# Partition sums of the conditioning products: a block transpose and a sum on the vector engine and three fold matmuls a layer, in place of two ones-column matmuls for each job

## The chip, the cores and the metric

The kernel runs on one core of one Trainium2 chip, as one launch. The metric is the device time of that launch in microseconds (us); lower is better. The median of before is 2668.92 us over 3 runs (2668.68 to 2669.47).

## The reference, cut to what matters

Two layers of a decoder trunk over 512 tokens of width 1024. In each layer three sub-layers (a gated feed-forward block, a mixer, a second gated feed-forward block) are modulated by a shift, a scale and a gate that come from one conditioning vector `c` of 1024 numbers:

```
c_act = jax.nn.silu(c)
for l in range(DEPTH):
    mod = c_act @ w_ada[l] + b_ada[l]
    sh1, sc1, g1, sh2, sc2, g2, sh3, sc3, g3 = jnp.split(mod, N_MOD, axis=-1)
    h = modulate(rmsnorm(x, norm_ffn1[l]), sh1, sc1)
    x = x + 0.5 * g1[:, None, :] * swiglu(h, ffn1_w_up[l], ffn1_w_down[l])
    h = modulate(rmsnorm(x, norm_mix[l]), sh2, sc2)
    x = x + g2[:, None, :] * hybrid_mixer(h, ...)
    h = modulate(rmsnorm(x, norm_ffn2[l]), sh3, sc3)
    x = x + 0.5 * g3[:, None, :] * swiglu(h, ffn2_w_up[l], ffn2_w_down[l])
```

`w_ada[l]` is 1024 x 9216 in float32. The change is only in how `c_act @ w_ada[l]` is summed.

## The kernel before, in words

The five engines have instruction streams written out by hand and meet at semaphores (`wait_ge`, `then_inc`); nothing reorders them. All activations are held with the 1024 features over the 128 partitions and the 512 tokens along the free axis. Each projection is made of units: one unit is one output tile of 128 features. Its weights arrive in `raw[s]` (s is 0 or 1, two units are a pair), the scalar engine rounds them to `Whi[s]` (L433), the vector engine makes the rest `Wlo[s]` (L703), and TensorE multiplies three times for each of the input tiles (L1179, L1180, L1181: high by high, high weights by low activations, low weights by high activations). A unit of the up projection has 8 input tiles (24 matmuls), one of the down projection 11 (33 matmuls).

A feed-forward block (`ffn(l, f)` on every engine, f is 0 for the first and 1 for the second) has two halves of `HALF` = 11 up pairs and then 4 down pairs. After an up pair VectorE multiplies the two banks (L810) and makes the low part of the product (L813); after each unit of a down pair it adds the bank into the residual stream (L787, `add_gated`).

The conditioning product is cut into jobs of 256 columns: 36 for a layer. The first 8 of layer 0 are made ahead of the layers, in code that the change leaves alone. The other 28 of a layer ride in the first feed-forward block: one behind each of the 11 up pairs and the first 3 down pairs, in both halves; and the first 8 of layer 1 ride in the second feed-forward block of layer 0. So 2 x 28 + 8 = 64 jobs are concerned. A job has these parts:

- the scalar engine issues the load of 1 MB of `w_ada` into `ada_raw` (L450);
- VectorE (`ada_sum_job`) multiplies its 8 row tiles by the columns of `c_act` and adds them into `ada_acc`, 128 partitions x 256 (L713 once, L715 seven times); what is left is a sum over the 128 partitions;
- TensorE (`ada_job`, placed behind the next pair of units) makes that sum with two matmuls of `ada_acc` by a column of ones, into two columns of PSUM (L1205);
- VectorE (`ada_store_job`, ahead of the sum of the next job) adds the bias and puts the two columns into `mod` (L726).

`mod` is read by `norm` (shift and scale) and by `halve_gate` (gate, L793). The last down pair of the second half is followed by the sum of squares of the next norm on TensorE (`sum_squares`, L1142), the inverse root on VectorE (L735 to L743), its spread over the partitions on TensorE (`spread_rstd`, L1212) and the norm itself (L778, L772).

## Time and profile before

| | |
|---|---|
| median of 3 runs | 2668.92 us (2668.68 to 2669.47) |
| span of the profiled execution | 2665.5 us from its first to its last instruction |
| TensorE matmuls busy | 2561.8 us, 96% of the span |
| VectorE busy | 1378.9 us, 52% |
| ScalarE busy | 849.9 us, 32% |
| GpSimd busy | 96.5 us, 4% |
| mean granted TensorE clock | 0.979 of full speed |

The profiled execution has its span; no device time of its own is listed beside it. The span leaves out what lies before the first and behind the last instruction: the median of the runs is 3.4 us above it. In rows of TensorE the ends of matmuls are modelled and overlap, so steps are best read from start to start.

### The profile page before, as it was taken

The page shows a single profiled execution, that of the slowest core. Times are in us where ns is not written, and L with a number is a line of the kernel's source. Part 1 is how long each engine was busy: PE and PEld are TensorE (multiplying, and loading weights), DVE is VectorE, ACT ScalarE, POOL GpSimd, SP SyncE. Part 2 cuts the span into 40 slices and gives each one's busy share as a digit, 9 for nine tenths or more (in the row PEclk, how much of TensorE's full clock was granted, in tenths as well). Part 3 has the DMA queues.
Part 4 walks back from the last instruction along what each step waited for, and adds up shares of the span by engine and source line. Part 5 has one row for each costly group of instructions (what it writes and reads, how often), then busy time and mean ns, then how long its engine had stood idle before and what let it go on. Part 6 is the DMA issues. An engine that isn't in the chain of part 4 may idle for free.

```text
span 2665.5 us, 36408 instructions
## 1 busy us (share of the span) xinstructions
PE 2561.8 (96%) x12039; PEld 2101.2 (79%) x12039; DVE 1378.9 (52%) x2175; ACT 849.9 (32%) x1276; POOL 96.5 (4%) x76
## 2 busy tenths in 40 slices
PE   6999999999999989999989999999999999899998
PEld 5888887877778878888868888877777888788886
DVE  7665665467644446433356656645665343433333
ACT  2321222444422334222222222234443223332222
POOL 3000001000000010000100000100000001000001
PEclk7999998999999999999989999999999999999999
DMA  6664664211123436423336656532111343233332
GB/s 220 181 194 137 186 179 132 79 56 55 56 63 100 129 90 186 120 85 99 106 103 180 181 160 183 164 103 64 55 55 48 94 128 101 71 102 95 95 109 65
DMA packets 494947, 307.08 MB, mean 115 GB/s; under 512 B 8904, under 2 KB 488472, under 8 KB 494232
## 3 DMA queue, kind: packets, MB, share of 16 engines
q1 hardware_dynamic: 427288, 239.03, 30.8%
q10 hardware_dynamic: 67584, 67.12, 7.8%
q8 instruction: 39, 0.64, 0.1%
q14 instruction: 36, 0.29, 0.0%
HBM read 299.82 MB, written 6.29 MB: 115 GB/s over the span
## 4 chain that ended last, share of the span: by engine, by line
PE 81%; DVE 9%; ACT 4%; issue 3%; DMA 1%; DVEq 0%; ACTq 0%; SPq 0%
PE ps_proj L1179 25%; PE ps_proj L1181 24%; PE ps_proj L1180 24%; ACT sb_scratch L534 2%; DVE sb_small L899 1%; DVE sb_w_lo L703 1%; DVE sb_scratch L896 1%; PE ps_mid L1322 1%; PE ps_mid L1324 1%; PE ps_mid L1323 1%; DVE sb_scratch L919 1%; ACT sb_w_hi L433 1%; PE ps_mid L1205 1%; PE ps_mid L1383 1%; DVE sb_scratch L924 1%
## 5 line engine op out<-in xcount | busy, mean ns | idle before, releaser
L1179 PE MATMUL ps_proj<-sb_h_hi,sb_w_hi 128*128 128x512 f32 x2048 | 815.0, 398 | 18.6 <-DVE sb_h_lo L772 14.4
L1181 PE MATMUL ps_proj<-sb_h_hi,sb_w_lo 128*128 128x512 f32 x2048 | 801.8, 392 | 0.0
L1180 PE MATMUL ps_proj<-sb_h_lo,sb_w_hi 128*128 128x512 f32 x2048 | 801.2, 391 | 0.0
L703 DVE TENSOR_TENSOR sb_w_lo<-sb_raw,sb_w_hi 128x1024 fp32r<-128x1024 f32 (+1 forms) x388 | 500.9, 1291 | 462.1 <-ACT sb_w_hi L433 454.0
L433 ACT ACTIVATE sb_w_hi<-sb_raw 128x1024 fp32r<-128x1024 f32 (+1 forms) x388 | 430.3, 1110 | 811.9 <-PE ps_proj L1181 755.3
L1179 PEld LDWEIGHTS ps_proj<-sb_h_hi,sb_w_hi 128*128 128x128 f32 x2048 | 386.9, 189 | 114.5 <-DVE sb_h_lo L772 20.2
L1181 PEld LDWEIGHTS ps_proj<-sb_h_hi,sb_w_lo 128*128 128x128 f32 x2048 | 386.8, 189 | 82.8
L1180 PEld LDWEIGHTS ps_proj<-sb_h_lo,sb_w_hi 128*128 128x128 f32 x2048 | 387.6, 189 | 78.0
L1179 PE MATMUL ps_proj<-sb_a_hi,sb_w_hi 128*128 128x512 f32 x1088 | 426.5, 392 | 0.0
L1181 PE MATMUL ps_proj<-sb_a_hi,sb_w_lo 128*128 128x512 f32 x1088 | 424.3, 390 | 0.0
L1180 PE MATMUL ps_proj<-sb_a_lo,sb_w_hi 128*128 128x512 f32 x1088 | 423.8, 390 | 0.0
L1181 PEld LDWEIGHTS ps_proj<-sb_a_hi,sb_w_lo 128*128 128x128 f32 x1088 | 204.6, 188 | 43.0
L1180 PEld LDWEIGHTS ps_proj<-sb_a_lo,sb_w_hi 128*128 128x128 f32 x1088 | 204.8, 188 | 42.2
L1179 PEld LDWEIGHTS ps_proj<-sb_a_hi,sb_w_hi 128*128 128x128 f32 x1088 | 204.6, 188 | 41.7
L715 DVE SCALAR_TENSOR_TENSOR sb_scratch<-sb_scratch,sb_c_act 128x256 f32<-128x256 f32 x448 | 217.2, 485 | 16.0
L787 DVE SCALAR_TENSOR_TENSOR sb_x_or_values<-ps_proj,sb_half_gate,sb_x_or_values 128x512 f32 (+1 forms) x80 | 60.1, 751 | 289.3 <-PE ps_proj L1181 288.7
L810 DVE TENSOR_TENSOR sb_scratch<-sb_scratch,ps_proj 128x512 f32<-128x512 f32 x88 | 60.5, 687 | 206.5 <-PE ps_proj L1181 206.5
L477 ACT ACTIVATE sb_scratch<-ps_proj 128x512 f32<-128x512 f32 x88 | 52.7, 599 | 300.6 <-PE ps_proj L1181 300.5
L394 POOL TENSOR_TENSOR sb_scratch<-sb_scratch 128x512 f32<-128x512 f32 x35 | 62.2, 1778 | 1998.8 <-ACT sb_scratch L444 1998.2
L534 ACT ACTIVATE sb_scratch<-sb_scratch,sb_small 128x256 f32<-128x256 f32 x128 | 63.0, 493 | 0.0
L813 DVE TENSOR_TENSOR sb_a_lo<-sb_scratch,sb_a_hi 128x512 f32 (+1 forms) x88 | 60.2, 684 | 0.0
L444 ACT ACTIVATE sb_scratch<-sb_x_or_values 128x512 f32<-128x512 f32 (+1 forms) x56 | 34.6, 621 | 74.9 <-DVE sb_x_or_values L787 55.2
(148 smaller groups left out, 1765.8 us busy)
## 6 DMA issues: line engine op xcount, KB each, us to landing
sb_raw<-in_ffn_w_up SPq DMA_DIRECT2D x176, 512.0 KB, 3.8
sb_scratch<-in_w_ada ACTq DMA_DIRECT2D x128, 512.0 KB, 4.3
sb_raw<-in_w_in SPq DMA_DIRECT2D x100, 512.0 KB, 3.8
sb_raw<-in_ffn_w_down SPq DMA_DIRECT2D x64, 704.0 KB, 4.5
sb_raw<-in_w_branch_swa SPq DMA_DIRECT2D x16, 512.0 KB, 3.6
sb_raw<-in_w_branch_ret SPq DMA_DIRECT2D x16, 512.0 KB, 3.6
sb_raw<-in_w_out SPq DMA_DIRECT2D x16, 512.0 KB, 3.6
sb_scratch<-in_w_ada SPq DMA_DIRECT2D x14, 512.0 KB, 7.9
```

The costliest lines, as they stand in the source:

```text
L394: pool.tensor_tensor(square_sum, square_sum, squares[:, k % 2, :], ALU.add).then_inc(sq_used, 1)
L433: act.activation(Whi[s][:, 0:n], raw[s][:, 0:n], ACT.Copy).then_inc(hi_ready, 1)
L477: act.activation(side, pA[0][:, :], ACT.Silu).then_inc(bank_free[0], 1)
L534: last = act.activation(p, p, ACT.Exp, bias=neg_m[w][:, n:n + 1], scale=HD ** -0.5, accum_out=row_sum[w][:, n:n + 1])
L703: dve.tensor_tensor(Wlo[s][:, 0:n], raw[s][:, 0:n], Whi[s][:, 0:n].bitcast(F), ALU.subtract).then_inc(lo_ready, 1)
L715: ins = dve.scalar_tensor_tensor(ada_acc, ada_raw[s][:, k % 4, :], col, ada_acc, ALU.mult, ALU.add)
L787: dve.scalar_tensor_tensor(XV[:, m, :], pA[s][:, :], half_gate[:, bass.ds(m, 1)], XV[:, m, :], ALU.mult, ALU.add).then_inc(bank_free[s], 1)
L810: dve.tensor_tensor(work, side, pA[1][:, :], ALU.mult).then_inc(bank_free[1], 1)
L813: dve.tensor_tensor(Alo[:, i, :], work, Ahi[:, i, :].bitcast(F), ALU.subtract).then_inc(act_lo, 1)
L1179: pe.matmul(bank, Whi[s][:, w], hi, start=first, stop=False)
L1180: pe.matmul(bank, Whi[s][:, w], lo, start=False, stop=False)
L1181: return pe.matmul(bank, Wlo[s][:, w], hi, start=False, stop=last)
```

## The change

In a job, VectorE now goes on behind its eight products: it transposes `ada_acc` in blocks of 32 x 32 into `ada_turned`, and sums each run of 32 (`reduce_sum`), which gives 8 columns for the job in `ada_part`. Each of these holds, on partition p, a partial sum over one group of 32 partitions. `ada_part` gathers the columns of many jobs. A fold matmul (`fold_jobs`) multiplies them by a constant 128 x 128 matrix `fold_rows` that has a one wherever two partitions agree modulo 32. So the four groups are added and each partition gets the result. The store (`ada_store`) picks the right column for each group of 32 partitions in four additions.

There are three folds in layer 0 and two in layer 1: `GATE_FOLD` for the 11 jobs of the up pairs of the first half (88 columns), between the two units of the first down pair; `REST_FOLD` for the other 17 (136 columns), between the two units of the last down pair of the second half, ahead of `sum_squares`; and in layer 0 `NEXT_FOLD` for the 8 jobs of the next layer (64 columns), behind the ninth up pair of the second feed-forward block. The constants grow by 128 columns (64 KB), which the first load brings in.

```diff
-            def ada_sum_job(l, q):
+            def ada_sum_job(l, q, slot):
...
                         ins.then_inc(ada_step, 1)
                         dve.wait_ge(ada_step, 6 * no + k - s + 1)
 
-            def ada_store_job(l, q, to, bias):
-                dve.wait_ge(ada_col, job_no(l, q) + 1)
-                dve.tensor_tensor(mod[:, bass.ds(2 * to, 2)], pC, vcols[:, bass.ds(64 + bias, 2)],
-                                  ALU.add).then_inc(mod_done, 1)
+                dve.wait_ge(ada_used, 2 * no + 4)
+                dve.transpose(ada_turned, ada_acc).then_inc(ada_turn, 1)
+                dve.wait_ge(ada_turn, no + 1)
+                dve.reduce_sum(ada_part[:, bass.ds(8 * slot, 8)], ada_turned.rearrange("p (j r) -> p j r", r=32), AX.X).then_inc(ada_part_done, 1)
+
+            def ada_store(fold, q, n, bias):
+
+                dve.wait_ge(ada_fold, fold + 1)
+                for a in range(4):
+                    rows = slice(32 * a, 32 * (a + 1))
+                    last = dve.tensor_tensor(mod[rows, 2 * q:2 * (q + n)], pC[rows, 0:8 * n].rearrange("p (x a) -> p x a", a=4)[:, :, a],
+                                             vcols[rows, bass.ds(64 + bias, 2 * n)], ALU.add)
+                last.then_inc(mod_done, 1)
...
                     if f == 0:
-                        up(0, UP_UNIT, lambda n: ada_sum_job(l, q0))
-                        with st.loop(1, HALF - 1, 0) as i:
-                            up(i, UP_UNIT, both_jobs)
-                        up(HALF - 1, DOWN_UNIT, both_jobs)
+                        with st.loop(0, HALF - 1, 0) as i:
+                            up(i, UP_UNIT, own_job)
+                        up(HALF - 1, DOWN_UNIT, own_job)
+                        if half == 0:
+                            ada_store(fold_no(l, GATE_FOLD), FIRST_JOBS, GATE_JOBS, MOD_TILES * l + 2 * FIRST_JOBS)
...
+                            if f == 0 and half and s == 0 and isinstance(j, int):
+                                rest = JOBS - FIRST_JOBS - GATE_JOBS
+                                ada_store(fold_no(l, REST_FOLD), JOBS - rest, rest, MOD_TILES * l + 2 * (JOBS - rest))
...
-            def ada_job(l, q):
-                pe.wait_ge(ada_used, 2 * job_no(l, q) + 4)
-                pe.wait_ge(mod_done, job_no(l, q) + 1)
-                for n in range(2):
-                    last = pe.matmul(pC[:, n:n + 1], ada_acc[:, P * n:P * (n + 1)], ones, start=True, stop=True)
-                last.then_inc(ada_col, 1)
+            def fold_jobs(fold, end, slot, n):
+
+                pe.wait_ge(ada_part_done, end)
+                pe.matmul(pC[:, 0:8 * n], fold_rows, ada_part[:, 8 * slot:8 * (slot + n)], start=True, stop=True).then_inc(ada_fold, 1)
...
-                        if f == 0:
-                            ada_job(l, q0 + i - 1)
...
-                        with pe.Fori(0, KT // 2) as j:
+                        down(0, lambda: None if f else fold_jobs(fold_no(l, GATE_FOLD), job_no(l, FIRST_JOBS + GATE_JOBS), 0, GATE_JOBS))
+                        with pe.Fori(1, KT // 2) as j:
                             down(j, lambda: None)
                     else:
-                        add_pairs(3 * l + (3 if f else 1), down)
+                        add_pairs(3 * l + (3 if f else 1), down, lambda: None if f else fold_jobs(
+                            fold_no(l, REST_FOLD), job_no(l, JOBS), GATE_JOBS, JOBS - FIRST_JOBS - GATE_JOBS))
```

What moves, in the order of instructions. On TensorE, at the end of the loop over the up pairs of the first half, before (L1205 is the job's two matmuls, L1202 and L1203 its two waits, L1250 the loop):

```order
L1181 MATMUL ps_proj<-sb_h_hi,sb_w_lo 128x512
L1202 ISA
L1203 REGISTER_ALU
L1205 MATMUL ps_mid<-sb_consts,sb_scratch 128x1 x2
L1250 REGISTER_ALU
L1250 COMPARE_AND_BRANCH
```

and in the changed kernel at the same place (L1198 to L1200 are the three products, L1271 the loop):

```order
L1200 MATMUL ps_proj<-sb_h_hi,sb_w_lo 128x512
L1271 REGISTER_ALU
L1271 COMPARE_AND_BRANCH
L1209 ISA
L1210 REGISTER_ALU
L1216 ISA
```

The pair is followed at once by the branch and the next pair; the job and its two waits are gone. The first fold stands between the two units of the first down pair (L1222 is its wait):

```order
L1198 MATMUL ps_proj<-sb_a_hi,sb_w_hi 128x512
L1199 MATMUL ps_proj<-sb_a_lo,sb_w_hi 128x512
L1200 MATMUL ps_proj<-sb_a_hi,sb_w_lo 128x512
L1222 ISA
L1223 MATMUL ps_mid<-sb_scratch,sb_consts 128x88
```

One matmul of 88 columns, with one wait, stands where two units followed each other directly.

On VectorE, in the loop over the up pairs, before, between the low part of the product (L813) and the first product of the job (L713):

```order
L813 ISA [waits act_hi]
L813 TENSOR_TENSOR sb_a_lo<-sb_scratch,sb_a_hi 128x512
L725 ISA
L726 ISA [waits ada_col]
L726 ISA
L726 TENSOR_TENSOR sb_mod<-ps_mid,sb_vector_cols 128x2
L711 ISA
L713 TENSOR_SCALAR sb_scratch<-sb_scratch,sb_c_act 128x256 [waits ada_in0]
```

and in the changed kernel at the end of the job (L729 is the last of the products, L739 the block transpose, L741 the sum), where before the loop ended behind the last product:

```order
L729 SCALAR_TENSOR_TENSOR sb_scratch<-sb_scratch,sb_c_act 128x256 [waits ada_step]
L738 REGISTER_ALU
L739 STREAM_TRANSPOSE sb_scratch<-sb_scratch 128x256 [waits ada_used]
L741 ISA [waits ada_turn]
L741 TENSOR_REDUCE sb_scratch<-sb_scratch 128x8
L250 REGISTER_ALU
L250 COMPARE_AND_BRANCH
```

The store of the job before is gone from the head of the job, and two instructions that each wait for the one before stand at its end. Behind the last job of the first half VectorE waits for the fold and stores 22 columns for each group of 32 partitions (L748), ahead of halving the gate (L816):

```order
L741 TENSOR_REDUCE sb_scratch<-sb_scratch 128x8 [waits ada_turn]
L748 ISA [waits ada_fold]
L748 TENSOR_TENSOR sb_mod<-ps_mid,sb_vector_cols 32x22
L748 ISA
L748 TENSOR_TENSOR sb_mod<-ps_mid,sb_vector_cols 32x22
L748 ISA
L748 TENSOR_TENSOR sb_mod<-ps_mid,sb_vector_cols 32x22
L748 ISA
L748 TENSOR_TENSOR sb_mod<-ps_mid,sb_vector_cols 32x22
L815 REGISTER_ALU
L816 TENSOR_SCALAR sb_half_gate<-sb_mod 128x8 [waits mod_done]
```

Before, only the halving stood here, with columns that had been stored several jobs earlier.

## Rows read from the trace of the kernel before

**Rows 1.** The page: span, busy time of TensorE, chain that ended last by engine
```profile
span 2665.5 us, 36408 instructions
...
PE 2561.8 (96%) x12039; PEld 2101.2 (79%) x12039; DVE 1378.9 (52%) x2175; ACT 849.9 (32%) x1276; POOL 96.5 (4%) x76
...
PE 81%; DVE 9%; ACT 4%; issue 3%; DMA 1%; DVEq 0%; ACTq 0%; SPq 0%
```

**Rows 2.** Groups of instructions of TensorE: busy us, mean ns, idle before
```profile
L1205 PE MATMUL ps_mid<-sb_consts,sb_scratch 128*128 128x1 f32 x256 | 31.9, 228 | 0.0
...
L1205 PEld LDWEIGHTS ps_mid<-sb_consts,sb_scratch 128*128 128x128 f32 x256 | 38.3, 190 | 5.1
```

**Rows 3.** Timeline of TensorE around one job: start us, us, engine, line
```profile
129.89 0.39 PE L1181 MATMUL ps_proj<-sb_h_hi,sb_w_lo 128*128 128x512 f32 x1
130.12 0.50 PE L1205 MATMUL ps_mid<-sb_consts,sb_scratch 128*128 128x1 f32 x4
130.48 0.48 PE L1179 MATMUL ps_proj<-sb_h_hi,sb_w_hi 128*128 128x512 f32 x1
130.79 0.39 PE L1180 MATMUL ps_proj<-sb_h_lo,sb_w_hi 128*128 128x512 f32 x1
```

**Rows 4.** Timeline of VectorE over one pair with a job
```profile
119.15 0.69 DVE L810 TENSOR_TENSOR sb_scratch<-sb_scratch,ps_proj 128x512 f32<-128x512 f32 x1 [2.70 <-PE ps_proj L1181]
...
122.23 3.61 DVE L715 SCALAR_TENSOR_TENSOR sb_scratch<-sb_scratch,sb_c_act 128x256 f32<-128x256 f32 x7
126.60 1.23 DVE L703 TENSOR_TENSOR sb_w_lo<-sb_raw,sb_w_hi 128x1024 fp32r<-128x1024 f32 x1 [0.76 <-ACT sb_w_hi L433]
130.52 0.69 DVE L810 TENSOR_TENSOR sb_scratch<-sb_scratch,ps_proj 128x512 f32<-128x512 f32 x1 [2.70 <-PE ps_proj L1181]
```

**Rows 5.** Timeline of VectorE over one pair without a job
```profile
1190.08 0.69 DVE L810 TENSOR_TENSOR sb_scratch<-sb_scratch,ps_proj 128x512 f32<-128x512 f32 x1 [2.76 <-PE ps_proj L1181]
...
1200.96 0.69 DVE L810 TENSOR_TENSOR sb_scratch<-sb_scratch,ps_proj 128x512 f32<-128x512 f32 x1 [2.76 <-PE ps_proj L1181]
```

**Rows 6.** Groups of instructions of VectorE by shape
```profile
L899 DVE TENSOR_REDUCE sb_small<-sb_scratch 128x4 f32<-128x1024 f32 x32 | 39.0, 1220 | 1.1
...
L1035 DVE TENSOR_TENSOR sb_scratch<-ps_mid,sb_consts 128x256 f32<-128x256 f32 x8 | 3.3, 417 | 2.0 <-PE ps_mid L1377 2.0
```

**Rows 7.** Timeline of VectorE, last job of the first up stage
```profile
190.74 0.15 DVE L726 TENSOR_TENSOR sb_mod<-ps_mid,sb_vector_cols 128x2 f32<-128x2 f32 x1
190.81 0.34 DVE L713 TENSOR_SCALAR sb_scratch<-sb_scratch,sb_c_act 128x256 f32<-128x256 f32 x1
191.19 3.61 DVE L715 SCALAR_TENSOR_TENSOR sb_scratch<-sb_scratch,sb_c_act 128x256 f32<-128x256 f32 x7
```

**Rows 8.** Timeline of TensorE, last matmul of that up stage
```profile
186.76 0.39 PE L1181 MATMUL ps_proj<-sb_h_hi,sb_w_lo 128*128 128x512 f32 x1
```

**Rows 9.** Timeline of VectorE, last job of the second half
```profile
423.00 1.32 DVE L713 TENSOR_SCALAR sb_scratch<-sb_scratch,sb_c_act 128x256 f32<-128x256 f32 x1
424.35 3.61 DVE L715 SCALAR_TENSOR_TENSOR sb_scratch<-sb_scratch,sb_c_act 128x256 f32<-128x256 f32 x7
```

**Rows 10.** Timeline of TensorE, last matmul before that job
```profile
419.54 0.39 PE L1181 MATMUL ps_proj<-sb_a_hi,sb_w_lo 128*128 128x512 f32 x1
```

**Rows 11.** Timeline of TensorE, sum of squares behind the second half
```profile
437.91 1.32 PE L1142 MATMUL ps_small<-sb_consts,sb_scratch 128*128 128x1 f32 x8 [0.35 <-ACT sb_scratch L444]
```

**Rows 12.** Timeline of TensorE, two waits in the mixer
```profile
529.44 0.92 PE L1285 MATMUL ps_mid<-sb_scratch 64*128 64x256 f32 x6 [2.16 <-DVE sb_small L908]
...
540.26 0.70 PE L1285 MATMUL ps_mid<-sb_scratch 64*128 64x256 f32 x4 [1.54 <-DVE sb_small L908]
```

**Rows 13.** Windows of TensorE behind these: us, busy (count), PEclk, DMA, GB/s
```profile
530.80:534.00 3.20, 3.20 (x9) 0.50 0.00 0
...
541.00:544.00 3.00, 3.00 (x16) 1.00 0.02 5
```

**Rows 14.** DMA issues: KB each, median us to landing
```profile
sb_consts<-in_consts SPq DMA_DIRECT2D x1, 1536.0 KB, 9.7
```

More of the change, by code:

```diff
@@ L815, in up @@
                             jobs(i)
-                    def store_job(n):
-                        ada_store_job(l, q0 + n, q0 + n, MOD_TILES * l + 2 * (q0 + n))
-                    def both_jobs(n):
-                        store_job(n - 1)
-                        ada_sum_job(l, q0 + n)
-                    def next_layers_jobs(n, store=True, add=True):
-                        with dve.If(l < DEPTH - 1):
-                            if store:
-                                ada_store_job(l, JOBS + n - 1, n - 1, nc.s_assert_within(
-                                    MOD_TILES * (l + 1) + 2 * (n - 1), MOD_TILES, MOD_TILES * DEPTH - 2,
-                                    skip_runtime_bounds_check_because="the last layer does not come here"))
-                            if add:
-                                ada_sum_job(l, JOBS + n)
@@ new lines, in next_layers_job @@
+                    def next_layers_job(n):
+                        with dve.If(l < DEPTH - 1):
+                            ada_sum_job(l, JOBS + n, n)
+                    if f == 0:
+                        with st.loop(0, HALF - 1, 0) as i:
[3 more added lines that the diff above has]
+                            ada_store(fold_no(l, GATE_FOLD), FIRST_JOBS, GATE_JOBS, MOD_TILES * l + 2 * FIRST_JOBS)
+                    elif half == 0:
+                        with st.loop(0, FIRST_JOBS, 0) as i:
+                            up(i, UP_UNIT, next_layers_job)
+                        up(FIRST_JOBS, UP_UNIT)
+                        with dve.If(l < DEPTH - 1):
+                            ada_store(fold_no(l, NEXT_FOLD), 0, FIRST_JOBS, nc.s_assert_within(
+                                MOD_TILES * (l + 1), MOD_TILES, MOD_TILES * (DEPTH - 1),
+                                skip_runtime_bounds_check_because="the last layer does not come here"))
@@ L1217, in _, with add_pairs, between @@
             first_columns(4).then_inc(first_col, 1)
-            def add_pairs(no, pair):
+            def add_pairs(no, pair, fold=lambda: None):
+                def between():
+                    fold()
+                    sum_squares(no, 0)
                 with pe.Fori(0, KT // 2 - 1) as j:
                     pair(j, lambda: None)
-                pair(KT // 2 - 1, lambda: sum_squares(no, 0))
+                pair(KT // 2 - 1, between)
                 for part in (1, 2):
```

39 lines of the change are left out of this document (22 added, 17 removed).

## The prediction

> **What bounds the kernel now.** I read the page first: TensorE's matmuls are busy for 96% of a span of 2665.5 us, and 81% of the chain that ended last is its own work [rows 1]. So what TensorE no longer does counts in full, as long as nothing else comes to hold it. Then I read the groups of TensorE for the job's matmuls: 256 records with no idle time before them [rows 2]. There are 64 jobs, so a job is four records (each float32 matmul shows as two), and TensorE never waited for a job's sum. The timeline shows how they stand in the stream: between the last product of one pair at 129.89 and the first of the next at 130.48 [rows 3].
>
> What a job costs is best read from start to start of one event that recurs once a pair. The product of the two banks on VectorE does: 119.15 to 130.52 with a job, 11.37 us; 1190.08 to 1200.96 without one, 10.88 us [rows 4, 5]. The pair is the same 48 matmuls in both, 0.227 us each. A job costs 0.49 us, more than the 0.36 us that its rows seem to take, since the next products start a little later too (0.31 us between the first two [rows 3]).
>
> **What the change removes.** Of the 64 jobs, 62 stand between two units. The last of each layer's stands ahead of the sum of squares, and there TensorE is held by ScalarE a moment later (0.35 us idle before 437.91 [rows 11]); removing its 0.36 us only lengthens that wait, so I count those two at nothing. The 62 give 62 x 0.49 = 30.4 us. That the pair really falls to 10.88 us without its job, and isn't held there by VectorE, ScalarE or loads, I take from the stages without jobs [rows 5], and check below against VectorE's longer job.
>
> The 64 stores on VectorE (0.15 us, of which the next instruction sees 0.07: 190.74 to 190.81 [rows 7]) are replaced by 5 x 4 small ones. VectorE is idle when they run, so they count only where they stand ahead of something late; see the folds.
>
> **What it adds to VectorE.** The trace has no block transpose. The nearest rows of 256 elements are the product with a constant table, 0.42 us [rows 6], and the scalar product, which goes faster, 0.34 us [rows 7]. I take 0.42; 0.34 is the lower bound, and the 1.22 us of a sum over 1024 elements [rows 6] the upper. Those two rows lie on one line, (1.22 - 0.42)/768 = 1.04 ns for each element, so I price the new sum of 256 at 0.42 us too. Each of the two waits for the instruction before it, about 0.03 us (seven dependent products take 3.61 us). Together a job grows by 0.90 us, 0.73 to 1.70 with the bounds.
>
> The Trainium skill (VectorE: DVE Perf Modes, The three transpose paths) gives 311 ns for a block transpose of 128 x 128 in bf16; an estimate from it, with one more element for each of its cycles, is 0.44 us for 256 columns, if float32 costs no more. The sum below would be 0.1 us worse by it. No row here shows it.
>
> Does that hide? In an up pair the job's products end at 122.23 + 3.61 = 125.84. VectorE then idles until 126.60, when ScalarE's half of the next weights is ready, and makes the low half until 127.83 [rows 4]. With the store gone, the longer job ends at 126.67; in the changed kernel ScalarE is 0.49 us earlier, so the low half starts then and ends at 127.90. The next pair would want these weights about 0.4 us ahead of its product of banks at 119.15 + 10.88 = 130.03, at 129.6. So 1.7 us are left, or 0.9 at the upper bound. The weights of the second unit are made ahead of the job. Down pairs are 4 us longer. So 60 of the 64 longer jobs cost nothing; the four that a fold waits for do.
>
> **The folds on TensorE.** A fold is one float32 matmul, two records instead of four, with 88, 136 or 64 columns instead of one. Half a job, 0.25 us, is the lower bound; a whole job, 0.49, the upper. I take 0.35, since more columns lengthen it a little. Five folds: 1.8 us.
>
> **The waits ahead of the folds.** This is what the change puts in the path. The first fold needs the sum of the eleventh job, and stands only one unit of 33 matmuls behind the last up pair. That pair's last product starts at 186.76 [rows 8]; without the job in between, the fold's first weight load (0.19 us, and it carries the wait [rows 2]) would start 33 x 0.227 = 7.48 us later, at 194.24. On VectorE the products of that job end at 191.19 + 3.61 = 194.80 [rows 7], 0.07 earlier without the store; plus 0.90 for transpose and sum and 0.1 for the signal gives 195.7. TensorE waits 1.5 us. The second fold is alike: the last product ahead of it is at 419.54 [rows 10], its load would start at 427.02. The last job's first product takes 1.32 us instead of 0.34, as it does in the down pairs of this half only, and its products end at 427.96 [rows 9]; so the sum is ready at 427.96 - 0.07 + 1.0 = 428.9, a wait of 1.9 us. Both stand in both layers: 2 x (1.5 + 1.9) = 6.8 us. The third fold, in layer 0 only, stands one whole pair of 10.88 us behind its last job, and doesn't wait.
>
> Queued behind these waits on TensorE is the second unit of the down pair, so the wait counts in full. On VectorE the wait for the fold (ahead of the four stores) holds the first addition into the residual stream and then the low half of the next weights: they come some 3 us later than now, and TensorE wants them at the end of the second unit, 7.5 us behind the fold. Hidden.
>
> **The start.** The first load of constants grows by 64 KB. At the rate of the big one, 1536 KB in 9.7 us [rows 14], that is 0.4 us of the transfers that the start waits for; between 0 and 0.4 I take 0.2.
>
> **The sum.** 30.4 - 1.8 - 6.8 - 0.2 = 21.6 us. The span becomes 2643.9; with the 3.4 us by which the median of the runs stands above the span, 2668.9 - 21.6 = 2647.3.
>
> **Rivals.**
>
> 1. *The clock falls at the fold waits.* In the mixer a wait of 2.16 us ahead of 529.44 is followed by a stretch at half clock (1.2 GHz) that covers 530.8 to 534.0; one of 1.54 us ahead of 540.26 is not, 541 to 544 is at full clock [rows 12, 13]. My waits, 1.5 and 1.9, lie between. The Trainium skill (TensorE: Matmul & The Clock Gate, The HAM clock gate) has the array's clock set by how busy it was just before; the trace agrees. A stretch like that one, 3.2 us at half clock, loses 1.6 us. If all four waits do it: 6.4 us more, 2653.7.
> 2. *No wait at the folds.* If the transpose and sum were nearly free and the jobs ran earlier, the 6.8 us would stay: 2640.5. Against it: the old job alone ends at 194.80, already 0.56 us later than the fold's load at 194.24.
> 3. *The pair does not get shorter.* Without the job TensorE would wait for weights instead, since each pair then moves its 1 MB of weights and the job's 1 MB in 10.88 us where rows 5 moved only the first. Then the 30.4 us don't come, while TensorE's waits would also cover the folds: 2668 to 2671, no change. Against it: TensorE's records show no wait behind any job pair now, and the job-less pairs leave VectorE 2.76 us idle.
> 4. *Slower: VectorE becomes the bound of the up pairs.* If transpose and sum took x us instead of 0.90, each job beyond x = 0.90 + 1.7 = 2.6 holds its pair. All is given back when 21.6 = 4 (x - 0.9) + 60 (x - 2.6), at x = 2.8 us; at 3.0, 2647.3 + 8.4 + 24.0 = 2679.7. It needs a block transpose of over 2.3 us, nearly twice the dearest row of four times the size.
>
> **How the numbers follow.** The forecast as summed has 0.68. Its own range: the transpose at its bounds changes four waits by -0.3 to +3.2; the folds by -0.5 to +0.7; the start by 0.2 either way. The starts of the six stages behind a norm run at half clock for a while, and how long depends on when they start; 21 us earlier they start at another moment, which I can't place: 2 us either way. Together 2644 to 2653.5. Rival 1 has 0.12 and ends in the same place or just above. Rival 2 has 0.07, rival 3 0.05, rival 4 0.04, and 0.04 is left for what I don't see. A range from 2641 to 2655 leaves out the last three, most of rival 2 and little else.
>
> A measurement of this kernel can tell about 0.2%, 5.3 us. Forecast, rivals 1 and 2 are all faster: with part of the rest 0.92. Within 0.2%: 0.04. Slower: 0.04.
>
> **What would show each step.** The product of the banks every 10.88 us in all up pairs; the busy time of VectorE 50 us higher (64 x 0.84, less the stores); the block transpose near 0.42 us; two groups of TensorE waits for the sum on VectorE, four in all, 1.5 and 1.9 us; five folds of two records. Wrong would be the prediction if pairs with a job stay above 10.88 us, if the transpose takes over 1 us, or if the clock's half-speed stretches grow in number within the down stages.

## The result and the profile after

The changed kernel takes 2647.45 us (median of 4 runs, 2646.18 to 2649.83), the kernel before in the same series 2669.01 (4 runs, 2668.68 to 2669.47). The ratio is 0.992, with a 95% interval of 0.9908 to 0.9932: faster by 0.8%, with the whole interval below 1. The prediction was 2647.3.

The page of the changed kernel, which answers to [rows 1]:

```profile
span 2645.3 us, 35817 instructions
...
PE 2538.1 (96%) x11793; PEld 2077.2 (79%) x11793; DVE 1431.3 (54%) x2259; ACT 852.0 (32%) x1276; POOL 94.4 (4%) x76
```

TensorE has 246 matmul records less (256 gone, 10 new) and is busy for 23.7 us less. VectorE is busy for 52.4 us more. The span fell by 20.2 us, in one execution of each; the medians of the runs are 21.6 us apart.

The groups of VectorE and TensorE for the new instructions, by shape (busy us, mean ns, idle before):

```profile
L739 DVE STREAM_TRANSPOSE sb_scratch<-sb_scratch 128x256 f32<-128x256 f32 x64 | 28.5, 446 | 2.2
...
L741 DVE TENSOR_REDUCE sb_scratch<-sb_scratch 128x256 f32 x60 | 25.2, 420 | 9.7 <-DVE sb_scratch L739 9.7
...
L1223 PE MATMUL ps_mid<-sb_scratch,sb_consts 128*128 128x136 f32 x4 | 1.0, 331 | 3.3 <-DVE sb_scratch L741 3.3
L1223 PE MATMUL ps_mid<-sb_scratch,sb_consts 128*128 128x88 f32 x4 | 0.9, 309 | 2.2 <-DVE sb_scratch L741 2.2
```

The block transpose takes 0.446 us and the sum 0.420 us. The timeline of VectorE over one pair with a job answers to [rows 4]:

```profile
105.59 0.69 DVE L833 TENSOR_TENSOR sb_scratch<-sb_scratch,ps_proj 128x512 f32<-128x512 f32 x1 [2.01 <-PE ps_proj L1200]
...
108.47 3.61 DVE L729 SCALAR_TENSOR_TENSOR sb_scratch<-sb_scratch,sb_c_act 128x256 f32<-128x256 f32 x7
112.11 0.45 DVE L739 STREAM_TRANSPOSE sb_scratch<-sb_scratch 128x256 f32<-128x256 f32 x1
112.71 0.42 DVE L741 TENSOR_REDUCE sb_scratch<-sb_scratch 128x256 f32 x1 [0.15 <-DVE sb_scratch L739]
113.24 1.23 DVE L717 TENSOR_TENSOR sb_w_lo<-sb_raw,sb_w_hi 128x1024 fp32r<-128x1024 f32 x1
116.47 0.69 DVE L833 TENSOR_TENSOR sb_scratch<-sb_scratch,ps_proj 128x512 f32<-128x512 f32 x1 [2.01 <-PE ps_proj L1200]
```

The product of the banks (L833) comes at 105.59 and again at 116.47, 10.88 us later, where it took 11.37 [rows 4]: now a pair with a job is as long as one without [rows 5]. VectorE still sits idle for 2.01 us ahead of it, waiting for TensorE.

The timeline of TensorE at the first fold, with the row of the last product ahead of it:

```profile
188.45 0.39 PE L1200 MATMUL ps_proj<-sb_a_hi,sb_w_lo 128*128 128x512 f32 x1
189.94 0.46 PE L1223 MATMUL ps_mid<-sb_scratch,sb_consts 128*128 128x88 f32 x2 [1.10 <-DVE sb_scratch L741]
190.18 0.48 PE L1198 MATMUL ps_proj<-sb_a_hi,sb_w_hi 128*128 128x512 f32 x1
190.50 0.39 PE L1199 MATMUL ps_proj<-sb_a_lo,sb_w_hi 128*128 128x512 f32 x1
```

and at the last fold, up to where the clock has fallen:

```profile
414.47 0.39 PE L1200 MATMUL ps_proj<-sb_a_hi,sb_w_lo 128*128 128x512 f32 x1
416.54 0.50 PE L1223 MATMUL ps_mid<-sb_scratch,sb_consts 128*128 128x136 f32 x2 [1.67 <-DVE sb_scratch L741]
416.87 0.95 PE L1161 MATMUL ps_small<-sb_consts,sb_scratch 128*128 128x1 f32 x8
...
418.63 0.63 PE L1198 MATMUL ps_proj<-sb_a_hi,sb_w_hi 128*128 128x512 f32 x1
419.06 0.63 PE L1199 MATMUL ps_proj<-sb_a_lo,sb_w_hi 128*128 128x512 f32 x1
```

What a fold costs with its wait is best read from starts: from 188.45 to the second product behind the fold at 190.50 are 2.05 us, where two steps of the stream would be 0.45, so the first fold costs 1.60. From 414.47 to the sum of squares at 416.87 are 2.40, where one step would be 0.23, so the last costs 2.17. The number in brackets is less (1.10 and 1.67), since the weight load of the fold is in the cost and not in the wait.

Behind the last fold the products start 0.43 us apart instead of 0.23. The windows of TensorE (us; busy and count of PE, PEld, DVE, ACT, POOL; granted clock; DMA share; GB/s) show why; the first row is behind the last fold of layer 0, the second follows it, and the third is behind the last fold of layer 1:

```profile
418.90:422.10 3.20, 3.20 (x9) 2.43 (x9) 0.08 (x1) 0.00 (x0) 0.00 (x0) 0.57 0.54 164
422.30:425.00 2.70, 2.70 (x13) 2.21 (x12) 0.00 (x0) 0.00 (x0) 0.00 (x0) 1.00 0.00 0
...
1709.30:1712.30 3.00, 3.00 (x10) 2.34 (x9) 0.28 (x2) 0.00 (x0) 0.00 (x0) 0.57 0.55 174
```

TensorE is busy without a gap in all three, but in the first and third the granted clock is near half: 9 or 10 matmuls are done there, where full clock does some 15. By the spacing of the products (0.43 us against 0.23), each such stretch loses about 1.6 us, an estimate. Behind the first fold, with a cost of 1.60 us, there is none.

The stages of both traces, in us, from the first spread of 1/rms on TensorE to the next; the start is all that comes ahead, and the time at half clock is the sum of the trace's clock records at that level:

| | start | ffn 1, layer 0 | mixer 0 | ffn 2, layer 0 | ffn 1, layer 1 | mixer 1 | ffn 2, layer 1 | half clock |
|---|---|---|---|---|---|---|---|---|
| before | 52.8 | 388.9 | 317.3 | 381.5 | 388.3 | 314.4 | 374.1 | 116.2 |
| after | 51.6 | 380.6 | 317.1 | 377.2 | 379.6 | 316.9 | 373.7 | 123.1 |
| change | -1.2 | -8.3 | -0.2 | -4.3 | -8.7 | +2.5 | -0.4 | +6.9 |

(The rest of each mixer, 216.5, and the end, 15.1, stayed within 0.2.) Three stages hold the jobs and are shorter by 21.3 us. The mixer of layer 1, in which nothing was changed, is 2.5 us longer.

### The profile page after: what moved, and what is told of

The parts are those of the page before. It is cut to its first block, busy times and chain, and to the rows that moved or that the text cites. A ratio compares the mean times of both kernels' runs of the same rounds, so it can differ in the third digit from the quotient of the medians.

```text
span 2645.3 us, 35817 instructions
## 1 busy us (share of the span) xinstructions
PE 2538.1 (96%) x11793; PEld 2077.2 (79%) x11793; DVE 1431.3 (54%) x2259; ACT 852.0 (32%) x1276; POOL 94.4 (4%) x76
## 4 chain that ended last, share of the span: by engine, by line
PE 79%; DVE 11%; ACT 5%; issue 3%; DMA 1%; DVEq 0%; ACTq 0%; SPq 0%
PE ps_proj L1198 24%; PE ps_proj L1199 24%; PE ps_proj L1200 24%; ACT sb_scratch L548 2%; DVE sb_w_lo L717 2%; DVE sb_small L918 1%; DVE sb_scratch L915 1%; PE ps_mid L1339 1%; ACT sb_w_hi L447 1%; PE ps_mid L1340 1%; PE ps_mid L1341 1%; DVE sb_scratch L938 1%; PE ps_mid L1400 1%; DVE sb_scratch L943 1%; DVE sb_scratch L729 1%
## 5 line engine op out<-in xcount | busy, mean ns | idle before, releaser
L1198 PE MATMUL ps_proj<-sb_h_hi,sb_w_hi 128*128 128x512 f32 x2048 | 810.3, 396 | 16.9 <-DVE sb_h_lo L795 12.7
L1200 PE MATMUL ps_proj<-sb_h_hi,sb_w_lo 128*128 128x512 f32 x2048 | 801.1, 391 | 0.0
L1198 PEld LDWEIGHTS ps_proj<-sb_h_hi,sb_w_hi 128*128 128x128 f32 x2048 | 386.7, 189 | 114.6 <-DVE sb_h_lo L795 18.4
L1200 PEld LDWEIGHTS ps_proj<-sb_h_hi,sb_w_lo 128*128 128x128 f32 x2048 | 386.9, 189 | 81.7
L1198 PE MATMUL ps_proj<-sb_a_hi,sb_w_hi 128*128 128x512 f32 x1088 | 426.8, 392 | 0.0
L1200 PE MATMUL ps_proj<-sb_a_hi,sb_w_lo 128*128 128x512 f32 x1088 | 425.9, 391 | 0.0
L1200 PEld LDWEIGHTS ps_proj<-sb_a_hi,sb_w_lo 128*128 128x128 f32 x1088 | 205.7, 189 | 43.3
L1198 PEld LDWEIGHTS ps_proj<-sb_a_hi,sb_w_hi 128*128 128x128 f32 x1088 | 205.8, 189 | 42.9
L729 DVE SCALAR_TENSOR_TENSOR sb_scratch<-sb_scratch,sb_c_act 128x256 f32<-128x256 f32 x448 | 217.3, 485 | 16.0
L833 DVE TENSOR_TENSOR sb_scratch<-sb_scratch,ps_proj 128x512 f32<-128x512 f32 x88 | 60.5, 688 | 181.7 <-PE ps_proj L1200 181.4
```

Of the source, the lines that this page charges most:

```text
L729: ins = dve.scalar_tensor_tensor(ada_acc, ada_raw[s][:, k % 4, :], col, ada_acc, ALU.mult, ALU.add)
L833: dve.tensor_tensor(work, side, pA[1][:, :], ALU.mult).then_inc(bank_free[1], 1)
L1198: pe.matmul(bank, Whi[s][:, w], hi, start=first, stop=False)
L1200: return pe.matmul(bank, Wlo[s][:, w], hi, start=False, stop=last)
```

## The experiments

Three theories on the size and place of the result: (A) the gain is TensorE's time for the jobs, 0.49 us each, and the waits at the folds are its price; (B) the folds' waits cost more than they show, since the clock falls behind them; (C) VectorE's longer job is near the bound. All ratios are to the kernel before, timed on the same chip.

**e0: the changed kernel again**, for comparison with e1 to e3.

> The changed kernel once more, beside its variants on one chip. My account (the 62 jobs leave TensorE's path, four waits ahead of the folds and two half-clock stretches are the price): 2647.4 us again, within 1.5, as the others of this call are read against it. A rival that calls the first result a lucky draw has it 5 us or more away.

Measured: 2647.48 us (5 runs, 2646.14 to 2648.67), ratio 0.992 (0.9906 to 0.9933).

**e1: the first fold takes only 4 jobs**, those that the gate needs; the other 24 go to the last fold.

```
-GATE_JOBS = HALF
+GATE_JOBS = 4
```

> The first fold takes only the 4 jobs that the gate needs (32 columns), the last fold the other 24 (192 columns). The first fold then needs a sum that was ready seven pairs earlier. If the wait of the first fold is a real cost on the path: its matmul follows the unit without a wait, about 1.25 us less in each layer, 2.5 us less than the changed kernel, 2645; the last fold and the half-clock stretch behind it stay. Rival (the time is only moved, since VectorE is late at that place anyway and its weights would hold the second unit): no difference, and a wait for low weights appears in the first down pair.

Measured: 2642.98 us (2641.63 to 2644.17), ratio 0.9903 (0.9888 to 0.9918), 4.5 us less than e0. Two rows of TensorE's timeline, the first fold and the last:

```profile
188.80 0.31 PE L1223 MATMUL ps_mid<-sb_scratch,sb_consts 128*128 128x32 f32 x2
...
415.26 0.59 PE L1223 MATMUL ps_mid<-sb_scratch,sb_consts 128*128 128x192 f32 x2 [1.67 <-DVE sb_scratch L741]
```

The first fold has no wait left and costs 0.24 us, so 2 x 1.36 = 2.7 us came from there, as expected. Of the other 1.8 us, about 1.6 are a half-clock stretch that is gone. The last fold still waits for 1.67 us, exactly as in the changed kernel, and yet of the windows behind it only that in layer 1 is at half clock:

```profile
418.70:422.00 3.30, 3.30 (x16) 2.75 (x15) 0.00 (x0) 0.00 (x0) 0.00 (x0) 1.00 0.38 140
1705.40:1708.40 3.00, 3.00 (x8) 2.31 (x7) 0.00 (x0) 0.00 (x0) 0.00 (x0) 0.50 0.59 175
```

The wait in layer 1 is the same 1.67 us. The same wait, with the same work ahead of it, is followed by half clock or not.

**e2: the last fold stands later**, between the second and the third part of the sum of squares, and its store ahead of the inverse root.

```
-                def between():
-                    fold()
-                    sum_squares(no, 0)
...
-                pair(KT // 2 - 1, between)
-                for part in (1, 2):
-                    sum_squares(no, part)
+                pair(KT // 2 - 1, lambda: sum_squares(no, 0))
+                sum_squares(no, 1)
+                fold()
+                sum_squares(no, 2)
```

> The last fold moves behind the last unit, between the second and third part of the sum of squares, where TensorE waits for ScalarE anyway; its store follows the last addition on VectorE. My account: in each layer the excess of 2.17 us at that fold goes, with the half-clock stretch behind it (1.6 us more), so about 7.5 us less than the changed kernel, 2640; the third part of the sum of squares starts no later behind the last unit than now. Rival (what is saved comes back in front of the norm, where fold, store and root would queue): the spread of the root starts 0.5 to 1.5 us later behind the last unit in each layer, and only 4 to 6 us are left.

Measured: 2641.5 us (2639.69 to 2642.2), ratio 0.9896 (0.9881 to 0.9911), 6.0 less than e0. TensorE's timeline at the last fold has no wait for VectorE's sum any more, and the window from the old place of the fold to the norm is at full clock throughout:

```profile
425.52 0.94 PE L1161 MATMUL ps_small<-sb_consts,sb_scratch 128*128 128x1 f32 x8
426.33 0.48 PE L1223 MATMUL ps_mid<-sb_scratch,sb_consts 128*128 128x136 f32 x2
427.27 0.94 PE L1161 MATMUL ps_small<-sb_consts,sb_scratch 128*128 128x1 f32 x7 [0.46 <-ACT sb_scratch L458]
```

```profile
417.00:430.50 13.50, 10.86 (x61) 9.20 (x59) 6.73 (x22) 3.27 (x4) 0.31 (x1) 1.00 0.13 39
```

The two stages of the first feed-forward blocks are 3.2 and 3.8 us shorter than in e0. The whole wait and fold would give 2.17 each, and a half-clock stretch 1.6: 3.8. The 0.6 us that layer 0 lacks lie at the start of the stage, as the table under e3 shows. The rival, that the saving comes back in front of the norm, is out: the spread of the root starts 5.55 us behind the last product in both layers, in e0 and in e2.

**e3: both edits.**

> Both edits: the fold of the gate with 4 jobs only, the last fold behind the last unit. If the two prices are apart from each other they add up: 2.5 and 7.5 us less than the changed kernel, 2637.5; TensorE then shows no wait for the sum on VectorE at any fold. If the clock at the starts of later stages takes its share, up to 3 us of it are lost.

Measured: 2639.87 us (2638.49 to 2640.64), ratio 0.9893 (0.9878 to 0.9908), 7.6 less than e0. No fold waits. The same two stages are 6.1 and 5.3 us shorter than in e0; the waits, folds and stretches account for 1.36 + 3.8 = 5.2 each. In layer 0 the time from the spread to the first product of the banks differs by up to 1.7 us between the traces, for the same instructions. Without it, from the first product of the banks of the first feed-forward block to the next spread, the traces agree with the account within 0.1 us, but for layer 1 of e1 (us):

| | layer 0 | layer 1 | shorter than in e0 | accounted for |
|---|---|---|---|---|
| before | 368.28 | 368.13 | | |
| after | 359.97 | 359.99 | | |
| e0 | 359.99 | 359.95 | | |
| e1 | 357.08 | 359.15 | 2.9, 0.8 | 1.36 + 1.6 = 3.0; 1.36 |
| e2 | 356.20 | 356.20 | 3.8, 3.8 | 3.8 each |
| e3 | 354.81 | 354.80 | 5.2, 5.2 | 5.2 each |

In layer 1 of e1 another half-clock stretch begins 3.6 us ahead of the spread, over the sum of squares, and the spread comes 6.04 us behind the last product instead of 5.55: that is the missing 0.5.

e4 to e7 ran on another chip, on which the kernel before took 2669.03 us instead of 2667.93, so differences to e0 and e3 below are uncertain by about 1 us more.

**e4: the matmuls of the jobs put back.** On the changed kernel, TensorE again makes two float32 ones-column matmuls for each job, at the old places, but on a constant tile, without a wait, into a bank that nobody reads. What the kernel computes stays the same.

```
+            def ones_pair():
+                for n in range(2):
+                    pe.matmul(pM[:, 0, n:n + 1], ident, ones, start=True, stop=True)
```

> The changed kernel with two ones-column matmuls put back on TensorE at each of the old places in the first feed-forward blocks and for the eight jobs of the next layer, on a constant tile into an unused bank, so that they wait for nothing and nobody waits for them. If the gain is the matmuls' own time on TensorE: 62 x 0.49 = 30.4 us more than the changed kernel, 2678, and every pair with a job back at 11.37 us. Rival (part of the gain came from the waits and stores that went with them, on TensorE's queue or on VectorE): less, 10 to 25 us.

Measured: 2675.96 us (10 runs, 2674.48 to 2677.54), ratio 1.0026 (1.0016 to 1.0035): slower than before the change, and 28.5 us above e0. VectorE's timeline has the product of the banks 11.38 to 11.39 us apart:

```profile
107.62 0.69 DVE L833 TENSOR_TENSOR sb_scratch<-sb_scratch,ps_proj 128x512 f32<-128x512 f32 x1 [2.52 <-PE ps_proj L1200]
119.00 0.69 DVE L833 TENSOR_TENSOR sb_scratch<-sb_scratch,ps_proj 128x512 f32<-128x512 f32 x1 [2.52 <-PE ps_proj L1200]
130.39 0.69 DVE L833 TENSOR_TENSOR sb_scratch<-sb_scratch,ps_proj 128x512 f32<-128x512 f32 x1 [2.52 <-PE ps_proj L1200]
```

So two matmuls of one column cost 0.51 us in each pair, although they do next to nothing, and they are the whole gain: 62 x 0.51 = 31.6 us. Less came for two reasons. TensorE arrives 0.5 us later at the folds, and the two cost 1.08 and 1.66 instead of 1.60 and 2.17, which gives back 2.1 us over two layers; and the half-clock stretch behind the last fold of layer 0 is gone, 1.6 us. That would leave 27.9. From the first product of the banks to the spread, layer 0 is 11.0 us and layer 1 12.7 us longer than in e0, where 27 x 0.51 less the folds, and in layer 0 less the stretch, gives 11.1 and 12.7. The clock again treats the two last folds differently: their waits are 1.16 and 1.17 us, and of the windows behind them (layer 1, then layer 0) the first is at half clock:

```profile
1737.20:1740.20 3.00, 3.00 (x8) 2.35 (x8) 0.50 (x3) 0.00 (x0) 0.00 (x0) 0.50 0.59 169
431.50:434.50 3.00, 3.00 (x15) 2.47 (x15) 1.13 (x5) 0.08 (x1) 0.00 (x0) 1.00 0.39 94
```

**e5: e3 and two more block transposes in each job**, each waiting for the one before, so that a job on VectorE grows by 0.96 us.

```
-                dve.transpose(ada_turned, ada_acc).then_inc(ada_turn, 1)
-                dve.wait_ge(ada_turn, no + 1)
+                for turn in range(3):
+                    dve.transpose(ada_turned, ada_acc).then_inc(ada_turn, 1)
+                    dve.wait_ge(ada_turn, 3 * no + turn + 1)
```

> The kernel with both folds moved, and two more block transposes in each job, each behind a wait for the one before: 1.0 to 1.2 us more on VectorE for each of 64 jobs, 64 to 77 us of busy time. My account (in a pair the longer job has 1.4 us of room before the next unit lacks weights, by the changed kernel's trace): no more than 1 us of difference, 2640. Rival (work on VectorE counts in proportion): 2650 or more.

Measured: 2634.8 us (2633.77 to 2635.95), ratio 0.987 (0.9853 to 0.9886). VectorE is busy with block transposes for 57 us more, as its group shows, and the pairs still take 10.88 us, with the idle time ahead of the product of banks down from 2.01 to 1.05:

```profile
L740 DVE STREAM_TRANSPOSE sb_scratch<-sb_scratch 128x256 f32<-128x256 f32 x192 | 85.5, 446 | 6.6
```

```profile
106.18 0.69 DVE L834 TENSOR_TENSOR sb_scratch<-sb_scratch,ps_proj 128x512 f32<-128x512 f32 x1 [1.05 <-PE ps_proj L1201]
...
117.06 0.69 DVE L834 TENSOR_TENSOR sb_scratch<-sb_scratch,ps_proj 128x512 f32<-128x512 f32 x1 [1.05 <-PE ps_proj L1201]
```

From the first product of the banks to the spread both layers take 355.0 us, against 354.8 in e3. The work is hidden, as expected; that the kernel was 5 us faster than e3 was not, and e8 to e10 take it up.

**e6: e3 and four more block transposes.** The same edit with `range(5)`; a job grows by 1.92 us, to 2.97 from the end of the products to the end of the sum.

> The same with four more block transposes, 2.0 to 2.4 us more for each job: beyond the room of 1.4 us. My account: each of the 52 up pairs behind which a job stands now lacks weights by 0.6 to 1.0 us, 30 to 50 us in all, 2670 to 2690, so slower than before the change; TensorE's waits are for the low half of the weights. Down pairs, which are 4 us longer, stay as they are. Rival (the room is larger, up to 2.7 us by the idle time of VectorE in a pair without a job): 2640 still.

Measured: 2656.14 us (2655.02 to 2657.74), ratio 0.9949 (0.9933 to 0.9966), 16.3 above e3. The chosen mechanism is there and the size was missed: 30 to 50 us and a time above that of the kernel before were expected. The four transposes added 1.92 us to a job and not 2.0 to 2.4, and the room was not 1.4 us but about 1.6 (an estimate: 1.92 less the 0.36 below). TensorE's waits have a new line, and its timeline shows one of them:

```profile
PE ps_proj L1199 <- DVE sb_w_lo L717: 13.8, 27, 1.7
```

```profile
117.06 0.39 PE L1201 MATMUL ps_proj<-sb_h_hi,sb_w_lo 128*128 128x512 f32 x1
117.82 0.49 PE L1199 MATMUL ps_proj<-sb_h_hi,sb_w_hi 128*128 128x512 f32 x1 [0.38 <-DVE sb_w_lo L717]
```

TensorE waits for the low half of the weights, which VectorE makes behind the job. Only every other pair does: the product of the banks comes at 106.91, 117.83, 129.40, 140.30, so 10.92, 11.57 and 10.90 us apart. The mean over two pairs is 11.24, 0.36 above 10.88. In the traces the three stages with jobs, from the first product of the banks to the spread, are together 18.6 us longer than in e3.

**e7: the changed kernel and two more block transposes**, with the first and last fold where the change put them.

> The changed kernel with its folds where they are, and two more block transposes in each job. Pairs keep 10.88 us; each of the four fold waits grows by 1.0 to 1.2 us, 4 to 5 us in all. The wait of the first fold is then 2.1 to 2.3 us instead of 1.1: if such a wait is what brings the clock down, half-clock stretches appear behind the first fold too, 1.6 us for each, and the time is 2653 to 2656. Rival (the clock falls behind the last fold for another reason, the sum of squares that follows it): no new stretch behind the first fold, 2651.5 to 2652.5.

Measured: 2660.45 us (6 runs, 2658.28 to 2660.93), ratio 0.9967 (0.9955 to 0.998), 13 above e0 and above both of the expected ranges. The four waits for the sum grew from 5.5 us together to 9.2:

```profile
PE ps_mid L1224 <- DVE sb_scratch L742: 9.2, 4, 2.6
```

The first fold costs 2.46 us now and the last 3.26 and 3.13, so 3.8 of the 13 us are wait. Half clock follows the last fold of layer 0 (for twice as long as in the changed kernel), the first fold of layer 1, and the last fold of layer 1, in this order:

```profile
419.40:426.00 6.60, 6.60 (x22) 5.54 (x22) 2.09 (x6) 0.63 (x1) 0.00 (x0) 0.50 0.28 79
1487.80:1491.00 3.20, 3.20 (x9) 2.42 (x9) 2.28 (x2) 0.00 (x0) 0.00 (x0) 0.50 0.37 120
1716.40:1719.60 3.20, 3.20 (x11) 2.62 (x11) 1.47 (x5) 0.42 (x1) 0.00 (x0) 0.50 0.32 66
```

Behind the first fold of layer 0, with the same cost of 2.46, the clock stays full. So half clock can follow a fold that has no sum of squares behind it, which answers the rival, and need not follow it. The mixers are 0.9 and 2.2 us longer than in the changed kernel, and the time at half clock is 136.6 us against 123.1. The waits, two half-clock stretches more (3.2) and the mixers add up to 10.1 us; the profiled execution, the fastest of the six, has a span 9.6 above that of e0. For the rest of the 13 I have no trace.

**e8, e9, e10: e3 and e5 again, and one more block transpose instead of two**, all on one chip, on where e5's 5 us came from.

> The kernel of e3 unchanged, so that it and e5's kernel are timed beside each other on one chip. If the 5 us between them belong to the kernels, 2639.9 us as before. If they were chance between two calls, it falls towards 2635 or e9 rises.

> The kernel of e5 unchanged. Theory: VectorE's extra 0.9 us in each job lies in its idle time, and what differs is where the half-clock stretches fall, which is fixed by the program's timing and so comes again: 2634.8 us, with less half-clock time in the trace than e8 (109 against 120 us). Rival: the difference is noise between calls, and both come out within 1.5 us of each other.

> e3 with one more block transpose in each job instead of two. If the gain came from the VectorE work itself it would lie halfway, near 2637.3. If it comes from where half-clock stretches fall, it need not lie between: anywhere from 2634 to 2641, and the half-clock time in the trace should go with the time, about 0.5 us for each us of it, with up pairs at 10.88 us in all three.

Measured: e8 2639.81 us (2639.68 to 2640.2), e9 2637.45, e10 2639.28. The medians of e9 and e10 say little, since their executions fall into two groups: e9 has 2634.88, 2635.29, 2639.62 and 2639.76, and e10 2635.67, 2638.78, 2639.79 and 2640.15. So neither of my two readings holds. The 5 us are not fixed by the program, and not small noise about one value: by these times, one and the same kernel takes one of two. The profiled execution of e8 is of the longer kind (span 2637.9), that of e10 of the shorter (2633.8), and their windows in and behind the mixer of layer 1 show the difference. First e8, then e10:

```profile
1800.30:1803.50 3.20, 3.16 (x11) 2.14 (x12) 0.00 (x0) 3.17 (x11) 0.00 (x0) 0.50 0.16 47
...
1810.40:1817.00 6.60, 5.84 (x29) 4.66 (x30) 4.19 (x13) 4.91 (x13) 0.00 (x0) 1.00 0.00 0
2022.20:2028.80 6.60, 6.60 (x20) 5.44 (x21) 3.50 (x14) 0.16 (x1) 0.00 (x0) 0.50 0.00 0
```

```profile
1800.30:1803.50 3.20, 3.20 (x18) 2.44 (x19) 0.00 (x0) 3.17 (x11) 0.00 (x0) 1.00 0.15 42
...
1810.40:1817.00 6.60, 5.93 (x17) 4.32 (x18) 4.19 (x13) 4.90 (x13) 0.00 (x0) 0.50 0.00 0
2022.20:2028.80 6.60, 6.60 (x35) 5.61 (x36) 3.51 (x14) 0.32 (x1) 0.00 (x0) 1.00 0.03 6
```

At the same moments of nearly the same program one is at half clock where the other is not. At 2022 TensorE has no gap, and 20 matmuls are done there at half clock instead of 35; the half-clock stretch at 1810 in e10 lies where TensorE has gaps even at full clock (5.84 of 6.60 us busy in e8). The mixer of layer 1 is 317.6 us in e8 and 314.6 in e10, 3.0 of the 4.1 us between the two spans. The executions of e5 and e9 that were profiled have the pattern of e10, that of e3 the pattern of e8. By their times, none of the eight runs of e3 and e8 (one kernel) is of the shorter kind, six of the eight of e5 and e9 (one kernel) are, and one of the four of e10. That suggests that the added work makes the shorter kind likelier. It is not shown: e3 and e5 ran on different chips, and on the chip that had all three kernels it is 0, 2 and 1 of four. No two traces of one kernel were kept, one of each kind, so that the mixer of layer 1 makes the two times is read from traces of different kernels.

## Why the prediction was right

The time, 2647.45 against 2647.3, agrees better than its terms deserve. By its own steps:

**The jobs, 62 x 0.49 = 30.4 us: right.** Pairs with a job fell from 11.37 to 10.88 us. e4 shows cause and size by itself: the matmuls put back cost 0.51 us a pair and 28.5 us in all. Rival 3 (the pair does not shorten) is out.

**VectorE's job, grown by 0.90 us: 0.15 too low in most jobs.** The transpose took 0.446 instead of 0.42 and the sum 0.420 as priced, but in the loops the sum starts 0.15 us behind the end of the transpose and the next instruction 0.11 behind the sum. From the end of the products at 112.08 it is 1.05 us to the end of the sum and 1.16 to the next instruction. The job that the first fold waits for is not in a loop; its sum starts 0.03 us behind its transpose:

```profile
188.99 0.45 DVE L739 STREAM_TRANSPOSE sb_scratch<-sb_scratch 128x256 f32<-128x256 f32 x1
189.47 0.42 DVE L741 TENSOR_REDUCE sb_scratch<-sb_scratch 128x8 f32<-128x256 f32 x1
```

Its products end at 188.95, so it is 0.94 us there, and the fold's matmul starts at 189.94, 0.05 behind the end of the sum; for this signal the prediction had taken 0.1 without a row. The estimate of 0.44 us from the page of the Trainium skill (VectorE: DVE Perf Modes, The three transpose paths) was the better one; the trace's 0.446 agrees with it. VectorE's busy time grew by 52.4 us, predicted 50 (its own terms, 64 x 0.84 less 64 x 0.15 and plus 20 small stores, give about 47).

**The room of 1.7 us in an up pair: right.** With a job that is 2.97 us longer than its products, e6 loses 0.36 us a pair, so the pairs are held from about 2.6 (an estimate, 2.97 less 0.36), which was the threshold predicted. Rival 4 (VectorE is the bound) has its mechanism shown, but its price was wrong in one factor: it counted 60 jobs, those in down pairs too, which the prediction itself had called 4 us longer. Only up pairs with a job are held, 22 in each layer and 8 more, 52 in all. 52 x 0.36 = 18.7 us agrees with the 18.6 of the traces and is close to the 16.3 of the medians, where the formula's 60 x 0.37 and the folds gave some 30. Break-even would have been at 2.86 us instead of 2.83; nothing in the forecast hung on it.

**Folds and waits, 1.8 + 6.8 = 8.6 us: 0.8 too high.** The four waits stand where they were predicted. With its fold the first costs 1.60 (predicted 1.5 + 0.35) and the last 2.17 (1.9 + 0.35), the fifth fold 0.25 without a wait. Together 2 x 3.77 + 0.25 = 7.8. With 0.25 for each fold the waits themselves are 1.35 and 1.92, so about 0.5 of the 0.8 is the price of five folds, 0.35 instead of 0.25. Columns count little: the 32 of e1's first fold cost 0.24, the 64 of the fifth fold 0.25, and the last fold with 192 columns (e1) costs 0.09 more than with 136. The slow first product of the last job is there too: VectorE's and GpSimd's timelines, in that order,

```profile
410.38 1.38 DVE L727 TENSOR_SCALAR sb_scratch<-sb_scratch,sb_c_act 128x256 f32<-128x256 f32 x1
411.80 3.61 DVE L729 SCALAR_TENSOR_TENSOR sb_scratch<-sb_scratch,sb_c_act 128x256 f32<-128x256 f32 x7
```

```profile
409.57 2.04 POOL L408 TENSOR_TENSOR sb_scratch<-sb_scratch 128x512 f32<-128x512 f32 x1 [4.31 <-ACT sb_scratch L458]
```

show that the product ends at 411.76, 0.15 us behind the end of GpSimd's addition at 411.61; elsewhere it takes 0.35. The Trainium skill (SBUF — State Buffer, Who interferes with whom) says that this kind of instruction can contend with GpSimd for a shared pair of ports that one of them holds for its whole instruction. The trace agrees: all six of these slow products of the changed kernel overlap such an addition. What it would be without the addition was not tried.

**Rival 1 (the clock falls at the fold waits): it did, at two of the four.** This is what the forecast left out. It gave it 0.12 as a case for all four waits; the outcome is a mixture of the two cases, 3.2 us at the last folds of both layers. More half-clock stretches within the down stages were one of the signs by which the prediction wanted to be called wrong; it came, although the total held. e2 shows that the wait is needed, by taking it away: both stretches are gone, 6.0 us less. e1, e4 and e7 show that the length of the wait does not decide alone: at the last folds, 1.67 us was followed by half clock in five of six places (the changed kernel, e0 and e1) and 1.17 us in one of two (e4), at the first fold 1.10 us in none of four (the changed kernel and e0) and the longer wait of e7 in one of two. What decides stays open. That the last fold has eight matmuls of one column directly behind it and the first has full ones may matter; it was not tried apart. Rival 2 (no wait) was not what happened, but e3 is a kernel without one: 2639.87, where 2640.5 was predicted for it.

**The start, 0.2 us longer: not seen, and of no weight.** It is 1.2 us shorter in this profile and between 51.6 and 52.9 in the eleven others, against 52.8 before. A stage that varies by 1.3 us can't show 0.2. The sign is that of one trace, so the term stays open.

**What evened out.** By rows the sum is 30.4 - 7.8 - 3.2 + 1.2 (start) - 2.5 (mixer 1) = 18.1; the span fell by 20.2. Most of the other 2.1 lie at the edges of the stages. From the spread to the first product of the banks the four feed-forward blocks together take 0.9 us less. From the last product to the spread it is 0.5 less in all, partly by the clock: before, the last eight matmuls of the first sum of squares took 1.32 us [rows 11], now 1.05:

```profile
428.64 1.05 PE L1161 MATMUL ps_small<-sb_consts,sb_scratch 128*128 128x1 f32 x8 [0.80 <-ACT sb_scratch L458]
```

The wait for ScalarE in this row grew from 0.35 to 0.80 us, as the prediction said of the two jobs that it counted at nothing. Between these edges the three stages with jobs are 8.0, 3.7 and 8.0 us shorter, where the terms give 7.9, 3.7 and 7.9: the account of the jobs, folds and stretches is complete. That the total fell on the prediction within 0.2 us is luck, all the more since the kernel before varied from 2666.7 to 2671.49 in the nine runs beside e0. The mixer of layer 1 has the same instructions in all kernels and took 314.4 to 319.1 us. For the changed kernel the cause is read off, not tested: it has half-clock stretches at 1810.9 and at 2032.7, of the kind that e8 has, and the kernel before has only one, at 1841.4, of the kind that e10 has. The forecast's "2 us either way" for stages that start at another moment was the right idea and too small: the mixer of layer 1 alone moved by 2.5, and the two times of one kernel lie 5 us apart.

The fastest versions that were run are e3 (2639.87 and, again, 2639.81) and e5 (2634.8 and, again, 2637.45 as a mixture). e3 is the one to keep: it beats the changed kernel by 7.6 us for reasons that its trace shows.

## What to carry to other kernels

In this dense stream a float32 matmul of one column cost about a quarter of a microsecond, so many small ones are worth batching into one, on an engine that has room for the preparation; read the room between the end of the other engine's work and the moment it is wanted, not from its busy share. When a batch replaces many small steps, its last input is the new wait: split it so that what is wanted early needs only inputs long finished, and put the rest behind work that is there anyway (here that was worth another 7.6 us, a third of the gain). A wait in the stream can cost more than itself: here half clock followed some of the waits and cost about 1.6 us each time. And differences under some 5 us in a kernel like this one, with its half-clock stretches behind waits, should be checked stage by stage before they are given a cause.

## What the runs showed of the hardware that I had not expected

- The granted clock seems not to be settled by the program alone. e9's kernel took 2634.9, 2635.3, 2639.6 and 2639.8 us in four runs; two traces of near-identical kernels (e8 and e10) differ by which stretches in one mixer run at 1.2 GHz. The Trainium skill (TensorE: Matmul & The Clock Gate, The HAM clock gate) says that one kernel can show different numbers of slow matmuls from run to run; the times agree with that, and here the two groups are 5 us, or 0.2%, apart.
- The length of a wait does not tell what the clock does behind it: 1.17 us ahead of the sum of squares was followed by 3 us at half clock in layer 1 of e4 and not in layer 0, and the longer wait at the first fold of layer 0 in e7 was not.
- When VectorE was made slightly too slow for the pairs (e6), TensorE's waits fell on every other pair, 10.9 and 11.6 us in turn, not evenly on each.
- The pair of float32 ones-column matmuls cost 0.51 us in the stream on a constant tile with no wait at all, as much as it did on the jobs' sums, and a single float32 matmul of 32 or 64 columns cost 0.24 to 0.25, no more than one of the pair.
